# Latent heads: the inverse roots spread over rows by one split-format product, high and low parts in rows 0 and 32 with zero rows between

## The chip, the cores and the metric

The kernel runs on one core of one Trainium2 chip. The metric is the device time of one launch in microseconds (us), lower is better. A core has five engines with queues of their own: PE (TensorE, matrix products; its weight loads are listed as PEld), DVE (VectorE), ACT (ScalarE), POOL (GpSimd) and SP (SyncE, which here only issues DMAs). They meet by semaphores. The tensor engine has two clock levels, 1.2 and 2.4 GHz; the profile gives the granted clock as a share of the full one, so 0.50 is 1.2 GHz and 1.00 is 2.4 GHz.

## The reference, cut to what matters

The program is two transformer blocks and a hybrid block on 512 tokens of width 1024, about 2.3 ms in all. The change is inside one mixer of the first block, the latent attention of 8 heads (64 plain and 32 rotated features a head, 96 in all):

```
q  = (rms_norm(c_q, cq_norm) @ w_uq).reshape(B, S, H, dn + dr)
kv = (rms_norm(c_kv, ckv_norm) @ w_ukv).reshape(B, S, H, dn + dv)
k  = concatenate([kv[..., :dn], broadcast_to(k_rope[:, :, None, :], (B, S, H, dr))], axis=-1)
v  = kv[..., dn:]
q  = rms_norm(q, q_norm)            # one inverse root per token and head, over 96 features
k  = rms_norm(k, k_norm)
q  = concatenate([q[..., :dn], rope(q[..., dn:], pos)], axis=-1)
k  = concatenate([k[..., :dn], rope(k[..., dn:], pos)], axis=-1)
return causal_block_attention(q, k, v).reshape(B, S, H * dv)
```

## The kernel before, in words

The program is a row of stages, each a block in which every engine has a list of its own; a stage ends when all engines are through, semaphores are cleared, and the next begins. Nothing of one stage overlaps with the next, apart from DMAs that nobody has waited for yet. Around the change stand three stages: the attention `ev_nsa` (during which SP loads the constants and weights of the next one, in `fill`), then `ev_latent_heads` (function `latent_heads`), then the attention `ev_mla`, which needs all that `latent_heads` leaves: queries in `xnT`, keys in `ev_km`, values in `ev_vm`.

In `latent_heads` features lie on partitions and the 512 tokens along the free axis. Products go one after another into the 8 banks of `PS`; product number n uses bank n % 8, and the semaphore `made` counts them. The order is written out by hand on each engine:

- PE: products 0 to 7 make raw q (four plain, two rotated) and two of k; product 8 sums the squares of q per head, with a 0/1 matrix `pick`, into 8 rows; 9 to 14 make the rest; product 15 sums the squares of k. Products 16 to 21 (`spread_out(0, w)`) take the 8 rows of inverse roots `rs` of q and spread them over 128 rows by the 0/1 matrix `spread`, one for each of the six tiles of q. Product 22 is the first tile of values (`value(0)`), 23 to 28 spread the roots of k (`spread_out(1, w)`), 29 to 31 are the other three tiles of values.
- ACT squares, copies k out of the banks, and for each of the two sums (`power`) takes exp(-0.5 ln(x)); at the end it copies the four value tiles (`take_v`).
- DVE refines each root by one Newton step (`newton`, three instructions on 8 rows), and multiplies: `qo` and `ko` are the rotated parts, `nope` the plain parts, two half-height instructions for each tile.
- SP moves the rotated rows from `qo` to `xnT` and from `ko` to `ev_km`, 8 DMAs each, and waits for all 16.
- A bank is used again only when its reader is done: `spread_out(1, m)` waits for `q_done`, `value(1)` for all of `nope` of q, `value(3)` for `k_roped`.

A product of two f32 operands appears as two matmul records. Elsewhere the kernel uses a split format: f32 data is rounded to fp32r (the high part), the rest (f32 minus high) is rounded to fp32r as the low part, and products run on fp32r operands, each one matmul record (`split_product`, L555 to L557). `low_alias` gives an fp32r tile that lies on the memory of the tile allocated last.

Of the kernel before, what the change touches and what calls it, by code (L numbers as in the profile page):

```python
# [26 lines left out]
P = 128  # L27
# [3 lines left out]
EPS = 1e-6  # L31
# [1650 lines left out]
NH, HD = 8, 64  # L1682
CMP_L, CMP_S = 32, 16
# [41 lines left out]
def head_of_row():  # L1725
# [7 lines left out]
    return pick  # L1733

# [12 lines left out]
def mixer_even(nc, C, D, x, xnT):  # L1747
    with ExitStack() as mem:
# [204 lines left out]
        pick, spread = sb("pick", [P, 6, NH]), sb("spread", [NH, 6, P])  # L1953
# [39 lines left out]
        with ExitStack() as m3:  # L1993
            km, vm = sb("km", [P, NH, SEQ], m3), sb("vm", [P, NT, 512], m3)
            filled = 16 * sum(1 + rows.shape[0] // P for rows in C.made_rows.values())
            latent_heads(nc, C, cq, ckv, kr, uq, ukv, gm, cosT, sinT, turn, pick, spread, xnT, km, vm, loaded, filled)
# [279 lines left out]
def latent_heads(nc, C, cq, ckv, kr, uq, ukv, gm, cosT, sinT, turn, pick, spread, qm, km, vm, loaded, filled):  # L2276

    N = MQK
    with ExitStack() as mem, stage(nc, "ev_latent_heads", "zeroed made squared q_copied k_copied q_cos k_cos k_sin k_turned q_sin "
# [29 lines left out]
        def _(pe):  # L2309
# [27 lines left out]
            def spread_out(i, w):  # L2337
                nc.tensor.matmul(bank(), spread[:, w], rs[:, i], start=True, stop=True).then_inc(s["made"], 1)
# [12 lines left out]
            sums = bank()[0:NH]  # L2351
# [18 lines left out]
            sums = bank()[0:NH]  # L2370
            for m in range(4):
                nc.tensor.matmul(sums, pick[:, m], sq[:, 6 + m], start=m == 0, stop=False)
            nc.tensor.matmul(sums, C.ones[0:ROT, 0:NH], sq[0:ROT, 10], start=False, stop=True).then_inc(s["made"], 1)

            pe.wait_ge(s["q_rstd"], 1)
# [25 lines left out]
        def _(act):  # L2401
# [7 lines left out]
            def power(n, i):  # L2409
                act.wait_ge(s["made"], n + 1)  # L2410
                nc.scalar.activation(rs[:, i], PS[0:NH, n % 8, :], ACT.Ln, bias=ec[0:NH, 0:1], scale=1.0 / N).then_inc(s["logged"], 1)
# [7 lines left out]
            act.wait_ge(s["zeroed"], 1)  # L2419
            for m in range(4):  # L2420
# [17 lines left out]
        def _(dve):  # L2438
            step = Steps(dve, s["steps"])

            def newton(n, i, done):
                dve.wait_ge(s["exped"], i + 1)
                y, t = rs[:, i], tt[:, i]
                step(nc.vector.scalar_tensor_tensor(out=t, in0=PS[0:NH, n % 8, :], scalar=N * EPS, in1=y, op0=ALU.add, op1=ALU.mult))
                step(nc.vector.scalar_tensor_tensor(out=t, in0=t, scalar=-0.5 / N, in1=y, op0=ALU.mult, op1=ALU.mult))
                nc.vector.scalar_tensor_tensor(out=y, in0=t, scalar=1.5, in1=y, op0=ALU.add, op1=ALU.mult).then_inc(done, 1)
# [1235 lines left out]
```

## Time and profile before

| | |
|---|---|
| median of three timed runs | 2325.05 us (2324.07 to 2329.28) |
| profiled execution, its time | 2320.53 us |
| profiled execution, its span | 2319.0 us |
| mean granted clock of the tensor engine | 0.935 |
| busy: PE / DVE / ACT / POOL | 89% / 55% / 43% / 8% of the span |
| the stage `latent_heads` | from 304.0 to about 360.0 us of the span |

Times in a trace count from the start of the span. A busy share is an average over stages with different limits. A timeline row gives start, duration and, in brackets, how long the engine had been idle and who ended it; a row with x12 covers twelve instructions in one stretch. Matmuls overlap with their neighbours in the pipeline, so the step from one to the next is shorter than the duration of one.

### The profile page before, as it was taken

The page shows a single profiled execution, that of the slowest core. Times are in us where ns is not written, and L with a number is a line of the kernel's source. Part 1 is how long each engine was busy: PE and PEld are TensorE (multiplying, and loading weights), DVE is VectorE, ACT ScalarE, POOL GpSimd, SP SyncE. Part 2 cuts the span into 40 slices and gives each one's busy share as a digit, 9 for nine tenths or more (in the row PEclk, how much of TensorE's full clock was granted, in tenths as well). Part 3 has the DMA queues.
Part 4 walks back from the last instruction along what each step waited for, and adds up shares of the span by engine and source line. Part 5 has one row for each costly group of instructions (what it writes and reads, how often), then busy time and mean ns, then how long its engine had stood idle before and what let it go on. Part 6 is the DMA issues. An engine that isn't in the chain of part 4 may idle for free. (4 is left out here: it accounts for less than half of the span.)

```text
span 2319.0 us, 31287 instructions
## 1 busy us (share of the span) xinstructions
PE 2068.7 (89%) x11611; PEld 1570.0 (68%) x11611; DVE 1285.5 (55%) x1814; ACT 994.2 (43%) x1308; POOL 185.8 (8%) x182
## 2 busy tenths in 40 slices
PE   7966898889999989997899999997898789686998
PEld 5743334668888877876777888786476359575776
DVE  3367746353133234444566666888367745525888
ACT  2135736342223222221566665774243643404774
POOL 0010000000000000000311010111112200002111
PEclk9978988989999999997899999999999789886999
DMA  8006101144144125002778777995320000126996
GB/s 249 6 14 237 47 10 45 37 127 123 43 122 127 37 83 194 1 37 83 256 269 282 278 270 281 370 391 216 88 73 28 12 1 1 74 84 174 399 373 258
DMA packets 220713, 336.29 MB, mean 145 GB/s; under 512 B 50413, under 2 KB 135309, under 8 KB 220606
## 3 DMA queue, kind: packets, MB, share of 16 engines
q1 hardware_dynamic: 213470, 314.53, 40.0%
q0 software_dynamic: 7136, 20.34, 2.3%
q8 instruction: 66, 1.08, 0.2%
q14 instruction: 41, 0.34, 0.0%
HBM read 306.82 MB, written 26.95 MB: 144 GB/s over the span
## 5 line engine op out<-in xcount | busy, mean ns | idle before, releaser
L1526 DVE TENSOR_TENSOR moe_pass_wL<-moe_pass_w,moe_pass_wH 128x2048 fp32r<-128x2048 f32 (+1 forms) x144 | 303.4, 2112 | 115.8 <-ACT moe_pass_wH L1450 111.3
L1450 ACT ACTIVATE moe_pass_wH<-moe_pass_w 128x2048 fp32r<-128x2048 f32 (+1 forms) x144 | 254.7, 1772 | 129.6 <-PE PS L557 97.2
L555 PE MATMUL PS<-moe_pass_wL,moe_pass_xgH 128*128 128x512 f32 (+1 forms) x384 | 148.3, 386 | 9.1 <-DVE moe_pass_xgL L1531 4.8
L1526 DVE TENSOR_TENSOR hm_pass_wL<-hm_pass_w,hm_pass_wH 128x2048 fp32r<-128x2048 f32 x60 | 135.9, 2288 | 34.8 <-ACT hm_pass_wH L1450 34.7
L555 PE MATMUL PS<-xnT_low,ffn_upH 128*128 128x512 f32 x352 | 140.3, 399 | 7.4 <-DVE xnT_low L873 7.1
L557 PE MATMUL PS<-moe_pass_wH,moe_pass_xgH 128*128 128x512 f32 (+1 forms) x384 | 143.5, 374 | 0.0
L556 PE MATMUL PS<-moe_pass_wH,moe_pass_xgL 128*128 128x512 f32 (+1 forms) x384 | 143.5, 374 | 0.0
L557 PE MATMUL PS<-ffn_xH,ffn_upH 128*128 128x512 f32 x352 | 139.9, 397 | 0.0
L556 PE MATMUL PS<-ffn_xH,ffn_up_low 128*128 128x512 f32 x352 | 138.4, 393 | 0.0
L1450 ACT ACTIVATE hm_pass_wH<-hm_pass_w 128x2048 fp32r<-128x2048 f32 x60 | 112.2, 1910 | 17.1 <-PEq L1340 6.0
L880 DVE TENSOR_TENSOR ffn_hT<-ffn_sg,PS 128x512 f32<-128x512 f32 x22 | 15.1, 688 | 167.7 <-PE PS L557 167.7
L839 ACT ACTIVATE ffn_sg<-PS 128x512 f32<-128x512 f32 x22 | 13.2, 599 | 187.8 <-PE PS L557 187.8
L555 PEld LDWEIGHTS PS<-moe_pass_wL,moe_pass_xgH 128*128 128x128 f32 x384 | 72.5, 189 | 28.5 <-issue 11.8
L555 PE MATMUL PS<-xnT_low,od_in_wH 128*128 128x512 f32 x192 | 77.3, 403 | 7.1 <-DVE od_W_low L689 7.1
L555 PEld LDWEIGHTS PS<-xnT_low,ffn_upH 128*128 128x128 f32 x352 | 66.6, 189 | 22.4 <-DVE ffn_up_low L858 7.3
L557 PEld LDWEIGHTS PS<-moe_pass_wH,moe_pass_xgH 128*128 128x128 f32 x384 | 72.6, 189 | 10.6
L556 PEld LDWEIGHTS PS<-moe_pass_wH,moe_pass_xgL 128*128 128x128 f32 x384 | 72.7, 189 | 9.4
L557 PEld LDWEIGHTS PS<-ffn_xH,ffn_upH 128*128 128x128 f32 x352 | 66.9, 190 | 15.9
L556 PEld LDWEIGHTS PS<-ffn_xH,ffn_up_low 128*128 128x128 f32 x352 | 66.7, 190 | 15.8
L556 PE MATMUL PS<-od_xH,od_W_low 128*128 128x512 f32 x192 | 76.7, 399 | 0.0
L555 PE MATMUL PS<-hm_pass_wL,hm_pass_xgH 128*128 128x512 f32 x160 | 65.3, 408 | 12.7 <-DVE hm_pass_wL L1526 7.1
L557 PE MATMUL PS<-od_xH,od_in_wH 128*128 128x512 f32 x192 | 75.7, 394 | 0.0
(841 smaller groups left out, 4868.6 us busy)
## 6 DMA issues: line engine op xcount, KB each, us to landing
moe_pass_w<-in_moe_w_down SPq DMA_DIRECT2D x40, 1024.0 KB, 4.9
moe_pass_w<-in_moe_w_gate SPq DMA_DIRECT2D x32, 1024.0 KB, 5.2
moe_pass_w<-in_moe_w_up SPq DMA_DIRECT2D x32, 1024.0 KB, 7.2
hm_pass_w<-in_exp_w_gate SPq DMA_DIRECT2D x40, 512.0 KB, 7.7
hm_pass_w<-in_exp_w_up SPq DMA_DIRECT2D x40, 512.0 KB, 6.9
hm_pass_w<-in_exp_w_down SPq DMA_DIRECT2D x40, 512.0 KB
od_W<-in_od_w_in SPq DMA_DIRECT2D x12, 1024.0 KB, 8.2
moe_pass_w<-in_moe_w_gate SPq DMA_DIRECT2D x16, 768.0 KB
```

The costliest lines, as they stand in the source:

```text
L555: nc.tensor.matmul(out, lh, rl, start=start, stop=False)
L556: nc.tensor.matmul(out, ll, rh, start=False, stop=False)
L557: return nc.tensor.matmul(out, lh, rh, start=False, stop=stop)
L839: nc.scalar.activation(sg[:, c % 2], PS[:, c % 2, :], ACT.Silu).then_inc(s["silu"], 1)
L880: nc.vector.tensor_tensor(hT[:, c], sg[:, c % 2], PS[:, 2 + c % 2, :], ALU.mult).then_inc(s["hidden"], 1)
L1450: nc.scalar.activation(wH[:, i % S, 0:n], w[:, i % R, 0:n], ACT.Copy).then_inc(s["high"], 1)
L1526: nc.vector.tensor_tensor(wL[:, i % S, 0:n], w[:, i % R, 0:n], f32(wH[:, i % S, 0:n]), ALU.subtract) \
```

## The change

The inverse roots are kept in 40 rows instead of 8: the 0/1 matrix `pick` now has 40 columns, in which columns 32 to 39 repeat columns 0 to 7, so `rs` holds the 8 roots twice, in rows 0 to 7 and 32 to 39, and rows 8 to 31 get the inverse root of the constant alone. `newton` gets two instructions more: rows 0 to 39 are rounded to fp32r in a new tile `both`, and then rows 32 to 39 of it are overwritten with f32 minus rounded. `both` is cleared first on POOL. The matrix `spread` now has 128 rows, with its 8 rows at 0 and at 32 and zeros elsewhere, and ACT rounds it once into `heads` at the start of the stage. Each of the twelve spreading products then is one product of two fp32r operands with 128 rows. On DVE the second `newton` stands after two of the four `nope` of q, not ahead of them. The two constants are loaded at their new sizes.

```diff
+def sums_twice():
+    pick = np.zeros((P, 6, SUMS), np.float32)
+    for a in (0, LOW):
+        pick[:, :, a:a + NH] = head_of_row()
+    return pick.reshape(P, 6 * SUMS)
+
+def spread_twice():
+    spread = np.zeros((P, 6, P), np.float32)
+    for a in (0, LOW):
+        spread[a:a + NH] = head_of_row().transpose(2, 1, 0)
+    return spread.reshape(P, 6 * P)
...
-        pick, spread = sb("pick", [P, 6, NH]), sb("spread", [NH, 6, P])
+        pick, spread = sb("pick", [P, 6, SUMS]), sb("spread", [P, 6, P])
+        heads = low_alias(nc, "ev_spread_high", [P, 6, P])
...
-        rs, tt, ec = sb("rs", [NH, 2, SEQ]), sb("tt", [NH, 2, SEQ]), sb("ec", [P, 1])
+        rs, tt, ec = sb("rs", [SUMS, 2, SEQ]), sb("tt", [SUMS, 2, SEQ]), sb("ec", [P, 1])
+        both = mem.enter_context(nc.sbuf_tensor("lh_both", [P, 2, SEQ], F32R))
+        high, low = slice(0, SUMS), slice(LOW, SUMS)
...
+            step(nc.gpsimd.memset(f32(both[:, :, :]), 0.0))
...
             def spread_out(i, w):
-                nc.tensor.matmul(bank(), spread[:, w], rs[:, i], start=True, stop=True).then_inc(s["made"], 1)
+                nc.tensor.matmul(bank(), heads[:, w], both[:, i], start=True, stop=True).then_inc(s["made"], 1)
...
+            pe.wait_ge(s["spread"], 1)
             pe.wait_ge(s["q_rstd"], 1)
             spread_out(0, 4)
...
             act.wait_ge(s["zeroed"], 1)
+            act.wait_ge(loaded["rope"], 80)
+            nc.scalar.activation(heads[:, :, :], spread[:, :, :], ACT.Copy).then_inc(s["spread"], 1)
...
-                nc.vector.scalar_tensor_tensor(out=y, in0=t, scalar=1.5, in1=y, op0=ALU.add, op1=ALU.mult).then_inc(done, 1)
+                step(nc.vector.scalar_tensor_tensor(out=y, in0=t, scalar=1.5, in1=y, op0=ALU.add, op1=ALU.mult))
+                dve.wait_ge(s["zeroed"], 2)
+                step(nc.vector.tensor_copy(both[high, i], y))
+                nc.vector.tensor_tensor(both[low, i], rs[low, i], f32(both[low, i]), ALU.subtract).then_inc(done, 1)
...
-            newton(15, 1, s["k_rstd"])
             for m in range(4):
                 nope(18 + m, 0, m, qr, qm, s["q_done"])
+                if m == 1:
+                    newton(15, 1, s["k_rstd"])
```

On DVE, in the second half of the stage, stands before the change (L2481 makes `qo`, L2444 to L2446 are `newton`, L2455 is `nope`, L2488 makes `ko`):

```order
L2481 TENSOR_TENSOR lh_qo<-lh_qa,PS 128x512 x2
L2444 SCALAR_TENSOR_TENSOR lh_tt<-PS,lh_rs 8x512
L2445 SCALAR_TENSOR_TENSOR lh_tt<-lh_tt,lh_rs 8x512
L2446 SCALAR_TENSOR_TENSOR lh_rs<-lh_tt,lh_rs 8x512
L2455 SCALAR_TENSOR_TENSOR xnT<-lh_qn,ev_gm,PS 64x512 x8
L2488 TENSOR_TENSOR lh_ko<-lh_ka,PS 128x512 x2
L2455 SCALAR_TENSOR_TENSOR ev_km<-lh_kn,ev_gm,PS 64x512 x8
```

And in the changed kernel, at the same place:

```order
L2508 TENSOR_TENSOR lh_qo<-lh_qa,PS 128x512 x2
L2482 SCALAR_TENSOR_TENSOR xnT<-lh_qn,ev_gm,PS 64x512 x4
L2468 SCALAR_TENSOR_TENSOR lh_tt<-PS,lh_rs 40x512
L2469 SCALAR_TENSOR_TENSOR lh_tt<-lh_tt,lh_rs 40x512
L2470 SCALAR_TENSOR_TENSOR lh_rs<-lh_tt,lh_rs 40x512
L2472 CAST lh_both<-lh_rs 40x512
L2473 TENSOR_TENSOR lh_both<-lh_rs,lh_both 8x512
L2482 SCALAR_TENSOR_TENSOR xnT<-lh_qn,ev_gm,PS 64x512 x4
L2516 TENSOR_TENSOR lh_ko<-lh_ka,PS 128x512 x2
L2482 SCALAR_TENSOR_TENSOR ev_km<-lh_kn,ev_gm,PS 64x512 x8
```

The second `newton` moved behind four of the eight half-height multiplications of q, and is two instructions longer.

On PE the order of the products stays; the last rows of the stage read before the change (L2372 and L2373 sum the squares of k, L2338 is `spread_out`, L2335 `value`):

```order
L2372 MATMUL PS<-lh_sq,ev_pick 8x512 x4
L2373 MATMUL PS<-lh_sq,ones 8x512
L2338 MATMUL PS<-lh_rs,ev_spread 128x512 x6
L2335 MATMUL PS<-ev_ukv,ev_latent 128x512
L2338 MATMUL PS<-lh_rs,ev_spread 128x512 x6
L2335 MATMUL PS<-ev_ukv,ev_latent 128x512 x3
```

And in the changed kernel:

```order
L2393 MATMUL PS<-lh_sq,ev_pick 40x512 x4
L2394 MATMUL PS<-lh_sq,ones 40x512
L2359 MATMUL PS<-lh_both,ev_spread_high 128x512 x6
L2356 MATMUL PS<-ev_ukv,ev_latent 128x512
L2359 MATMUL PS<-lh_both,ev_spread_high 128x512 x6
L2356 MATMUL PS<-ev_ukv,ev_latent 128x512 x3
```

Nothing moved here; the operands of the twelve spreading products changed, and the sums have 40 rows.

## Rows read from the trace of the kernel before

**Rows 1.** Windows over the stage: length, busy time (x instructions) of each engine, granted clock, DMA.

```profile
332.00:336.00 4.00, 4.00 (x10) 1.31 (x9) 1.31 (x2) 2.50 (x3) 0.00 (x0) 1.00 0.00 0
336.00:340.00 4.00, 4.00 (x6) 1.67 (x5) 3.81 (x7) 0.09 (x1) 0.00 (x0) 0.50 0.41 96
...
356.00:360.00 4.00, 3.38 (x4) 0.77 (x3) 0.00 (x0) 1.78 (x3) 0.00 (x0) 0.52 0.00 0
```

**Rows 2.** Timeline of PE from the first spreading product to the next stage.

```profile
333.37 8.06 PE L2338 MATMUL PS<-lh_rs,ev_spread 8*128 8x512 f32 x12
341.35 2.08 PE L2335 MATMUL PS<-ev_ukv,ev_latent 128*128 128x512 f32 x2
343.36 10.61 PE L2338 MATMUL PS<-lh_rs,ev_spread 8*128 8x512 f32 x12
353.89 5.49 PE L2335 MATMUL PS<-ev_ukv,ev_latent 128*128 128x512 f32 x6
360.86 2.62 PE L391 MATMUL PS<-ev_km,xnT 96*128 96x128 f32 x10 [1.48 <-PEq L42]
363.59 0.33 PE L404 MATMUL PS<-ident,ev_mla_pn 128*128 128x128 f32 x1
```

**Rows 3.** Timeline of DVE in the same stage.

```profile
330.05 1.22 DVE L2477 TENSOR_TENSOR lh_qa<-lh_qa,lh_qb 128x1024 f32<-128x1024 f32 x1
334.59 1.48 DVE L2481 TENSOR_TENSOR lh_qo<-lh_qa,PS 128x512 f32<-128x512 f32 x2 [3.32 <-PE PS L2338]
336.12 0.68 DVE L2444 SCALAR_TENSOR_TENSOR lh_tt<-PS,lh_rs 8x512 f32<-8x512 f32 x1
...
338.16 6.18 DVE L2455 SCALAR_TENSOR_TENSOR xnT<-lh_qn,ev_gm,PS 64x512 f32<-64x512 f32 x8
...
354.00 1.52 DVE L2455 SCALAR_TENSOR_TENSOR ev_km<-lh_kn,ev_gm,PS 64x512 f32<-64x512 f32 x2 [0.18 <-PE PS L2338]
```

**Rows 4.** Timeline of ACT in the same stage.

```profile
306.98 0.63 ACT L2422 ACTIVATE lh_sq<-lh_qn 128x512 f32<-128x512 f32 x1 [9.47 <-DVE lh_qn L2460]
...
335.46 0.63 ACT L2413 ACTIVATE lh_rs<-lh_rs 8x512 f32<-8x512 f32 x1
...
359.42 0.60 ACT L2417 ACTIVATE ev_vm<-PS 128x512 f32<-128x512 f32 x1 [1.11 <-PE PS L2335]
```

**Rows 5.** SP's DMA issues (timeline), and from issue to landing for L2304.

```profile
224.79 10.29 SPq L1980 DMA_DIRECT2D hm_pass_made<-ev_TcT  x8
346.25 4.95 SPq L2304 DMA_DIRECT2D ev_km<-lh_ko  x8
DMA to landing us min/median/max: 1.9/2.0/2.1
```

**Rows 6.** Timeline of PE in an earlier stage: neighbouring products of fp32r operands.

```profile
60.10 0.39 PE L555 MATMUL PS<-xnT_low,ev_ring 128*128 128x512 f32 x1
60.33 0.39 PE L556 MATMUL PS<-ev_yT_low,ev_W_low 128*128 128x512 f32 x1
```

**Rows 7.** Groups by line and shape: busy us, mean ns of one, idle before.

```profile
L2262 DVE COPY xnT<-ev_front 64x2048 f32<-64x2048 f32 x1 | 1.2, 1225 | 0.0
L617 DVE TENSOR_TENSOR ev_yT_low<-ev_yT,ev_out_yH 128x512 fp32r<-128x512 f32 x8 | 5.5, 686 | 1.4 <-ACT ev_out_yH L596 1.4
L673 ACT ACTIVATE ev_ring<-ev_W 128x1024 fp32r<-128x1024 f32 x11 | 11.6, 1057 | 64.5 <-PE PS L557 64.5
L2295 POOL MEMSET xnT<- 32x2048 f32 x1 | 1.8, 1797 | 0.1
```

**Rows 8.** Start of the attention `ev_nsa`: PE's timeline, and a window with its clock.

```profile
188.11 4.84 PE L391 MATMUL PS<-ev_front,xnT 128*128 128x128 f32 x10 [2.29 <-PEq L42]
192.78 0.27 PE L404 MATMUL PS<-ident,ev_nsa_pn 128*128 128x128 f32 x1
188.00:192.00 4.00, 3.89 (x8) 2.62 (x9) 2.60 (x9) 1.31 (x5) 0.00 (x0) 0.50 0.53 160
```

**Rows 9.** A window inside the attention `ev_mla`.

```profile
384.00:388.00 4.00, 2.30 (x10) 1.12 (x11) 3.37 (x12) 3.52 (x12) 0.00 (x0) 0.90 0.00 0
```

More of the change, by code:

```diff
@@ L1682 @@
 NH, HD = 8, 64
+LOW, SUMS = 32, 40
 CMP_L, CMP_S = 32, 16
@@ L1995, in mixer_even @@
             filled = 16 * sum(1 + rows.shape[0] // P for rows in C.made_rows.values())
-            latent_heads(nc, C, cq, ckv, kr, uq, ukv, gm, cosT, sinT, turn, pick, spread, xnT, km, vm, loaded, filled)
+            latent_heads(nc, C, cq, ckv, kr, uq, ukv, gm, cosT, sinT, turn, pick, spread, heads, xnT, km, vm, loaded, filled)
             jobs = []
@@ L2273, in _, with latent_heads @@
             nc.vector.tensor_copy(pcT[:, :, :], PS[:, 6:8, :])
-def latent_heads(nc, C, cq, ckv, kr, uq, ukv, gm, cosT, sinT, turn, pick, spread, qm, km, vm, loaded, filled):
+def latent_heads(nc, C, cq, ckv, kr, uq, ukv, gm, cosT, sinT, turn, pick, spread, heads, qm, km, vm, loaded, filled):
     N = MQK
-    with ExitStack() as mem, stage(nc, "ev_latent_heads", "zeroed made squared q_copied k_copied q_cos k_cos k_sin k_turned q_sin "
+    with ExitStack() as mem, stage(nc, "ev_latent_heads", "zeroed spread made squared q_copied k_copied q_cos k_cos k_sin k_turned q_sin "
                                    "q_turned logged exped steps q_rstd k_rstd q_roped k_roped q_done k_done v_taken moved") as (block, s):
@@ L2350, in _ @@
             pe.wait_ge(s["q_copied"], 1)
-            sums = bank()[0:NH]
+            sums = bank()[high]
             for w in range(6):
@@ L2369, in _ @@
             pe.wait_ge(s["squared"], 11)
-            sums = bank()[0:NH]
+            sums = bank()[high]
             for m in range(4):
                 nc.tensor.matmul(sums, pick[:, m], sq[:, 6 + m], start=m == 0, stop=False)
-            nc.tensor.matmul(sums, C.ones[0:ROT, 0:NH], sq[0:ROT, 10], start=False, stop=True).then_inc(s["made"], 1)
+            nc.tensor.matmul(sums, C.ones[0:ROT, high], sq[0:ROT, 10], start=False, stop=True).then_inc(s["made"], 1)
+            pe.wait_ge(s["spread"], 1)
             pe.wait_ge(s["q_rstd"], 1)
@@ L2410, in power @@
                 act.wait_ge(s["made"], n + 1)
-                nc.scalar.activation(rs[:, i], PS[0:NH, n % 8, :], ACT.Ln, bias=ec[0:NH, 0:1], scale=1.0 / N).then_inc(s["logged"], 1)
+                nc.scalar.activation(rs[:, i], PS[high, n % 8, :], ACT.Ln, bias=ec[high, 0:1], scale=1.0 / N).then_inc(s["logged"], 1)
                 act.wait_ge(s["logged"], i + 1)
@@ L2443, in newton @@
                 y, t = rs[:, i], tt[:, i]
-                step(nc.vector.scalar_tensor_tensor(out=t, in0=PS[0:NH, n % 8, :], scalar=N * EPS, in1=y, op0=ALU.add, op1=ALU.mult))
+                step(nc.vector.scalar_tensor_tensor(out=t, in0=PS[high, n % 8, :], scalar=N * EPS, in1=y, op0=ALU.add, op1=ALU.mult))
                 step(nc.vector.scalar_tensor_tensor(out=t, in0=t, scalar=-0.5 / N, in1=y, op0=ALU.mult, op1=ALU.mult))
-                nc.vector.scalar_tensor_tensor(out=y, in0=t, scalar=1.5, in1=y, op0=ALU.add, op1=ALU.mult).then_inc(done, 1)
+                step(nc.vector.scalar_tensor_tensor(out=y, in0=t, scalar=1.5, in1=y, op0=ALU.add, op1=ALU.mult))
+                dve.wait_ge(s["zeroed"], 2)
+                step(nc.vector.tensor_copy(both[high, i], y))
+                nc.vector.tensor_tensor(both[low, i], rs[low, i], f32(both[low, i]), ALU.subtract).then_inc(done, 1)
             def gained(dst, src, col, other_):
@@ L3633 @@
 CONSTANTS = {"bucket_table": bucket_table, "rope_table": rope_tables, "rope_spread": rope_spread,
-             "head_pick": lambda: head_of_row().reshape(P, 6 * NH),
-             "head_spread": lambda: head_of_row().transpose(2, 1, 0).reshape(NH, 6 * P),
+             "head_pick": sums_twice, "head_spread": spread_twice,
              "ones_row": lambda: np.ones((1, NH), np.float32), "wkv_masks": wkv_masks, "chunk_restart": chunk_restart}
```

## Prediction, made before the changed kernel ran

> **What bounds the kernel now.** I read the timeline of the stage first, because a stage with a barrier behind it is worth exactly the time of whichever engine is last in it. PE is that engine. From its first spreading product at 333.37 it has no gap until the last value product [rows 2], and in the windows from 332 to 340 it is busy 4.00 of 4.00 us [rows 1]. DVE, which has as much to do with its multiplications, ends at 354.00 + 1.52 = 355.52 [rows 3]; ACT takes the last value tile from 359.42 to 360.02 [rows 4], and that is the end of the stage. The next stage's first product follows 0.84 us later, at 360.86 [rows 2].
>
> Then the clock. In 332 to 336 the granted clock is 1.00, in 336 to 340 it is 0.50, and it is still 0.52 in 356 to 360 [rows 1]: the engine ran at 1.2 GHz from about 336 on although it never paused. What it did ahead of the fall were products with 8 rows of operand (8\*128, 8x512). What it did ahead of the rise, which must lie at about 360 since the next stage starts at full speed, were products with 128 rows. The price is plain: six spreading products are 12 records and cost 333.37 to 341.35, 7.98 us, in the first group, which began at 2.4 GHz, and 343.36 to 353.89, 10.53 us, in the second, all at 1.2 GHz (1.75 each) [rows 2]. One value product costs 2.01 us there (341.35 to 343.36), the last three 5.49 [rows 2]. DVE waits for PE: at the last tile of k it had 0.18 us of idle time ahead of it [rows 3].
>
> So the end hangs on 12 spreading products (18.5 us) and 4 value products (7.5 us), on a PE at half clock. The rest of the program lies behind a barrier and moves with the end of this stage.
>
> **The change, part by part.**
>
> *Spreading products.* Two neighbouring fp32r products stand 0.23 us apart at full clock (60.10, 60.33) [rows 6]. Their cost does not depend on the rows used: the 8-row records here are as far apart as those of the 128-row values (1.75 for two records against 5.49 / 3 = 1.83 with the tail). So twelve products fall from 18.5 us to 12 x 0.23 = 2.8 us at full clock, or double that, 5.5 us, at half. PE stops being the last engine, and what matters is who is next: DVE.
>
> *First Newton step.* It gains a rounding of 40x512 and a subtraction of 8x512. The subtraction is a TENSOR_TENSOR of 512 elements per row, 0.69 us [rows 7]. No row rounds to fp32r on DVE. The lower bound is a plain copy from SBUF at 1.225 us for 2048 elements, a quarter of which is 0.31; the upper is that it runs like the TENSOR_TENSOR, 0.69 [rows 7]. I take 0.45, nearer the copy, as it has one source and a fixed part. With 0.05 for the two hand-overs the step is longer by about 1.2 us. The DVE work behind it, which ended at 330.05 + 1.22 = 331.27 [rows 3], then ends at 332.5. The spreading starts at 333.37, as PE is busy until then, so this is hidden with 0.9 us to spare; at the upper bound still with 0.7. The roots of q are ready earlier still on the same list, so they are hidden too.
>
> *The constant rounded on ACT.* 128x768: between 128x512 and 128x1024 at 1.057 us [rows 7], so about 0.8 us. ACT has nothing to do until 306.98 [rows 4], the stage opens at 304.0: free, 2 us to spare. If the cover were gone it would cost its 0.8.
>
> *POOL.* The memset of 1024 elements per row costs about half of 1.797, 0.9 us [rows 7]. The two memsets behind it end near 308.7 instead of 307.8, and their rows are first written by others at 334 and later. Free.
>
> *Loads.* `pick` grows from 128x48 to 128x240 values, `spread` from 8x768 to 128x768: 24 + 24 KB become 120 + 384 KB, under half a megabyte more. They stand early in the load queue of `ev_nsa`; all of its transfers are issued by 224.79 + 10.29 = 235.1 [rows 5], 69 us ahead of the stage. SP issues as many DMAs as before. Free.
>
> *40 instead of 8 rows or columns.* ACT and DVE instructions take their time from the elements per row (8x512 takes 0.68, as 128x512 does [rows 3]), and the matmuls stream the same 512 columns. Zero.
>
> *The new chain on DVE.* The first `qo` started 334.59 - 333.37 = 1.22 us after its product did, for two records [rows 2, 3]. One record less is half of that: 0.6, so `qo` starts at 333.97. From there I add, with durations of [rows 3]:
>
> - two `qo`, 1.48: to 335.45
> - four `nope` halves, 6.18 / 2 = 3.09: to 338.54
> - second Newton step; its input from ACT is there at 335.46 + 0.63 = 336.09 [rows 4], so no wait. 338.16 - 336.12 = 2.04, plus 1.2: to 341.78
> - four `nope` halves, 3.09: to 344.87
> - two `ko`, TENSOR_TENSOR like the `qo` and the one of [rows 7], 1.40: to 346.27
> - eight `nope` halves of k, 4 x 1.53 = 6.12: to 352.4
>
> DVE does not wait in between: the k spreading begins when `k_rstd` comes at 341.8, six products at 0.46 each are made by 344.6, and the first is needed at 344.87. The last of them and `value(1)` wait for the last `nope` of q, 344.87.
>
> *The others' ends.* PE: three value products from 344.9, at half clock 5.49 us, to 350.4, and 0.9 us more for ACT to take the last: 351.3. SP: first `ko` at 345.6, the last issue some 4.3 us on, landing 2.0 us later [rows 5]: 351.9. DVE is last at 352.4. Moving the Newton step behind two tiles of q costs nothing, as the chain is one list on one engine; it only makes k later (341.8 and not 338.7) and q earlier.
>
> *Sum in the stage.* 360.02 - 352.4 = 7.6 us less.
>
> *What is given back.* PE now idles from about 336 (six products and one value product) to 341.8, and again from 350.4 to the next stage at 352.4 + 0.84 = 353.2. Before, the last value products ran on until 359.4 and the attention opened at 2.4 GHz: from its first product to its first transposition 363.59 - 360.86 = 2.73 us. The other attention, `ev_nsa`, opened at clock 0.50, and there the same stretch took 192.78 - 188.11 = 4.67 us [rows 8]. The difference, 1.94 us, is my price of a cold opening; it is a little high, as `ev_nsa` has more work for DVE in a unit. I expect the cold opening.
>
> Here a rule of the Trainium skill ("TensorE: Matmul & The Clock Gate", "Why this matters for your kernels") can be weighed: idle gaps between bursts bring the half clock, and a busy engine is released from it. For the kernel before the trace does not agree with the second half: 4.00 of 4.00 us busy at 0.50. By the rule alone the kernel before would have had no half clock here to lose, and the change, which makes gaps, could only lose by it.
>
> **Sum.** 7.6 - 1.9 = 5.7 us. The profiled execution goes from 2320.53 to 2314.8. The median of the timed runs lies 4.5 us above the profiled one, so against it: 2325.05 - 5.7 = 2319.4 us, 0.25% less.
>
> **The rivals.**
>
> 1. *More is given back than a cold opening* (chance 0.30, time 2321 to 2325, no change that can be told). For it: the attention itself pauses often enough to lose the clock now and then; in 384 to 388 PE was busy 2.30 of 4.00 us and the mean clock was 0.90, so it fell inside the window [rows 9], and everything behind the stage is shifted by some 6 us against whatever sets these falls. If the cold opening lasts twice as long, 3.8 us go, and 3.8 are left. Against it: in `ev_nsa` it was over within 4.7 us.
> 2. *The attention opens warm* (chance 0.12, time 2317.4). The three values run 5.2 us on 128 rows without a pause, the same thing that stood ahead of the rise at 360, and only 3 us of idling follow. Then all 7.6 us stay.
> 3. *Slower, by a cold attention* (chance 0.05, time about 2334 at worst). One mechanism: the attention, entered at 1.2 GHz, does not get out. A cold us costs 1.94 / 4.67 = 0.42 us; the 7.6 us are used up after 18 us of cold attention, and with 40 us of it cold the loss is 17, so 9 us slower. For it: the clock stood at 0.50 in this stage under a busy engine [rows 1]. Against it: those were 8-row operands, and the attention's have 96 or 128 rows; `ev_nsa`, entered at 0.50, got out. The same page of the Trainium skill ("A second HAM failure mode: psum-queue depth-cycling") describes a kernel whose short idles between groups make the clock go back and forth; the trace agrees that this attention has such a fall [rows 9].
> 4. *The change does little, since PE was not what the end hung on* (chance 0.04, time 2324). DVE would end at 352.4 only if nothing holds it; if the rounding or the wait for cleared rows cost 3 us more than I think, 3 us of the gain go. The rows speak against it: 2 us of slack at each place.
>
> **How the numbers follow.** My forecast, 5.7 us less with a cold opening, has 0.49. A measurement of this kernel tells about 0.2% (4.65 us) from no change. Faster by more: forecast and rival 2, less a part for scatter about the bound that is only 1 us away: 0.58. Within 0.2%: rivals 1 and 4 and that part: 0.37. Slower: 0.05. The forecast's own range is rounding 0.31 to 0.69 (0.14 us and 0.24 us to either side, in one place on the path), opening 1.2 to 2.7: 2318.5 to 2320.4. To hold 8 in 10 it must reach to rival 2 and through rival 1, and carry the scatter of the timed runs (1 us below, 4 us above their median): 2315.5 to 2325.
>
> **What the changed profile would show.** Right: spreading products of one record, 0.23 to 0.46 us apart; DVE without a wait from 334 to 352.4, and last in the stage; PE idle from 336 to 342; the next stage's first product at 353.2 instead of 360.86; clock 0.50 in its first us and 1.00 within 5. Wrong: DVE waiting for PE anywhere behind 334; the rounding at more than 0.7 us; PE waiting for DVE ahead of 333.4; a clock that stays at 0.50 behind 360; or, in the sum, a part of the gain that is there at the end of this stage and gone at the end of the program.

## The result, and the profile after

The changed kernel takes 2310.61 us (median of 5 runs, 2303.26 to 2312.46); the kernel before, in turn with it, 2324.07 (5 runs, 2315.34 to 2329.28). The ratio is 0.9942, 95% interval 0.9917 to 0.9967. That is faster by 0.6%, where I had forecast 0.25% and a range whose fast end was 2315.5 us. The profiled execution took 2310.61, its span is 2309.1 at a mean granted clock of 0.937; before it was 2319.0.

First the stage of the change. PE's timeline of the changed kernel (start, length, line, operands, count, [idle before <- releaser]):

```profile
333.28 1.67 PE L2359 MATMUL PS<-lh_both,ev_spread_high 128*128 128x512 f32 x6
334.79 1.02 PE L2356 MATMUL PS<-ev_ukv,ev_latent 128*128 128x512 f32 x2
341.54 2.93 PE L2359 MATMUL PS<-lh_both,ev_spread_high 128*128 128x512 f32 x6 [5.73 <-DVE lh_both L2473]
344.66 3.52 PE L2356 MATMUL PS<-ev_ukv,ev_latent 128*128 128x512 f32 x6 [0.19 <-DVE xnT L2482]
352.90 5.03 PE L391 MATMUL PS<-ev_km,xnT 96*128 96x128 f32 x10 [4.71 <-PEq L42]
357.72 0.42 PE L404 MATMUL PS<-ident,ev_mla_pn 128*128 128x128 f32 x1
```

The spreading products are single records and take 1.67 and 2.93 us where they took 8 and 10.5 [rows 2]. From the second group on PE waits for DVE and no longer the other way round. DVE's timeline:

```profile
326.40 0.42 DVE L2472 CAST lh_both<-lh_rs 40x512 fp32r<-40x512 f32 x1
326.86 0.68 DVE L2473 TENSOR_TENSOR lh_both<-lh_rs,lh_both 8x512 fp32r<-8x512 f32 x1
...
333.89 1.28 DVE L2508 TENSOR_TENSOR lh_qo<-lh_qa,PS 128x512 f32<-128x512 f32 x2 [1.46 <-PE PS L2359]
335.09 3.08 DVE L2482 SCALAR_TENSOR_TENSOR xnT<-lh_qn,ev_gm,PS 64x512 f32<-64x512 f32 x4
...
344.63 1.28 DVE L2516 TENSOR_TENSOR lh_ko<-lh_ka,PS 128x512 f32<-128x512 f32 x2
345.84 6.19 DVE L2482 SCALAR_TENSOR_TENSOR ev_km<-lh_kn,ev_gm,PS 64x512 f32<-64x512 f32 x8
```

The rounding costs 0.42 us, DVE runs without a wait from 333.89 to 352.03 and is last. The next stage's first product starts at 352.90 instead of 360.86 [rows 2]. The windows with the granted clock (length, busy and count of PE, PEld, DVE, ACT, POOL, then clock, DMA share, GB/s):

```profile
336.00:340.00 4.00, 0.00 (x0) 0.00 (x0) 3.83 (x6) 0.49 (x2) 0.00 (x0) 0.91 0.46 108
340.00:344.00 4.00, 2.46 (x6) 1.82 (x6) 3.80 (x7) 0.00 (x0) 0.00 (x0) 0.50 0.07 17
344.00:348.00 4.00, 3.81 (x8) 1.41 (x6) 3.90 (x6) 1.19 (x2) 0.00 (x0) 0.74 0.20 47
348.00:352.00 4.00, 0.18 (x1) 0.00 (x0) 3.84 (x6) 0.60 (x1) 0.00 (x0) 1.00 0.36 85
352.00:356.00 4.00, 3.10 (x7) 2.27 (x8) 1.58 (x7) 1.11 (x5) 0.00 (x0) 0.61 0.50 173
356.00:360.00 4.00, 4.00 (x11) 2.38 (x10) 2.86 (x12) 2.67 (x8) 0.00 (x0) 0.53 0.90 339
360.00:364.00 4.00, 2.98 (x15) 1.65 (x14) 3.18 (x10) 4.00 (x14) 0.00 (x0) 1.00 0.05 18
```

The attention opens at 1.2 GHz, and from its first product to its first transposition are 4.82 us (352.90 to 357.72) where there were 2.73. So far all is as forecast. Here the gain is 363.59 - 357.72 = 5.87 us. A part of it, 0.2 us, was there ahead of the stage: from the stage's first product to the attention's it takes 48.87 us where it took 56.66, 7.79 us less.

To see where the other 5 us come from I subtracted the start times of the same DVE instruction in two profiles, all along the program. Each row begins with the place in the kernel before; the numbers are the shifts of the others against it, each from one profile (the kernels are those of the next section; "before again" is a second profile of the kernel before):

```
place (us)                     after   again1  again2  old order  awake  delay  f32rows  before again
 294.9 ahead of the stage      -0.2    -0.5    -1.7    -1.2       -1.2   +1.1   -1.0     +0.6
 365.9 attention has begun     -5.9    -6.3    -7.6    -6.1       -8.7   +2.9   -7.3     +0.6
 486.6 attention is over       -7.2    -7.6    -9.0    -7.6       -7.9   +1.4   -6.5     +0.6
1941.2                         -3.5    -8.9    -8.7    -4.1      -11.6   +5.0   -1.1     +0.3
2085.5 router of the last MoE  -9.7   -14.0   -15.2   -10.9      -12.4   -1.8   -1.7     +0.5
```

Between 486 and 1941 shifts come and go by up to 5.4 us, in either direction. Between 1941 and 2085 they don't scatter: five of the six kernels with the split format gain 5.1 to 6.8 us there (9.7 - 3.5 = 6.2 in the changed kernel), in code that the change doesn't touch, and the two with f32 products in this table 0.6 or less. Behind 2085 the shifts drift again: from there to the last DVE instructions (at 2314.9 in the kernel before) the changed kernel gains 0.2 us more, and the others of this table lose 0 to 3.9 us. The timeline of that router before (L195 transposes the tokens, L204 multiplies with the router's weights):

```profile
2065.62 2.24 SPq L2652 DMA_DIRECT2D hm_br<-in_router_eb  x1
2070.39 4.87 DVE L179 SCALAR_TENSOR_TENSOR hm_xs<-x,hm_norm_ss,hm_gx 128x1024 f32<-128x1024 f32 x4 [4.33 <-DMA hm_br<-in_router_eb]
2071.74 3.68 PE L195 MATMUL PS<-ident,hm_xs 128*128 128x128 f32 x16 [4.39 <-DVE hm_xs L179]
2075.21 3.44 PE L204 MATMUL PS<-hm_wr,xnT 128*128 128x20 f32 x16
2080.22 3.44 PE L204 MATMUL PS<-hm_wr,xnT 128*128 128x20 f32 x16
```

and after:

```profile
2062.10 0.81 SPq L2680 DMA_DIRECT2D hm_br<-in_router_eb  x1
2065.62 4.87 DVE L179 SCALAR_TENSOR_TENSOR hm_xs<-x,hm_norm_ss,hm_gx 128x1024 f32<-128x1024 f32 x4 [3.03 <-DMA hm_br<-in_router_eb]
2066.95 3.34 PE L195 MATMUL PS<-ident,hm_xs 128*128 128x128 f32 x16 [3.08 <-DVE hm_xs L179]
2070.13 1.94 PE L204 MATMUL PS<-hm_wr,xnT 128*128 128x20 f32 x16
2072.87 1.86 PE L204 MATMUL PS<-hm_wr,xnT 128*128 128x20 f32 x16
```

The issue of one small load takes 0.81 us instead of 2.24, the token scaling that waits for it starts 3.52 us behind that issue instead of 4.77, and then the same sixteen products take 1.94 and 1.86 us instead of 3.44. Their windows, before:

```profile
2070.00:2074.00 4.00, 2.26 (x11) 2.27 (x12) 3.61 (x4) 0.26 (x1) 0.00 (x0) 0.50 0.94 259
2074.00:2078.00 4.00, 4.00 (x21) 4.00 (x20) 1.27 (x2) 1.92 (x4) 0.00 (x0) 0.50 0.97 355
```

and after:

```profile
2066.00:2070.00 4.00, 3.04 (x15) 3.05 (x16) 4.00 (x4) 1.04 (x2) 0.00 (x0) 0.57 0.98 259
2070.00:2074.00 4.00, 4.00 (x38) 4.00 (x37) 1.18 (x2) 1.73 (x4) 0.00 (x0) 1.00 1.01 409
```

What lengthens the issue? The DMA queues over the 2.3 us from that issue on, in the kernel before (2065.6 to 2067.9; packets, MB, share):

```profile
q1 hardware_dynamic: 2157, 0.12, 62.3%
q8 instruction: 1, 0.02, 2.5%
```

and over the 2.9 us from it on in the changed one (2062.1 to 2065):

```profile
q1 hardware_dynamic: 2354, 0.31, 74.9%
```

A load of instructions falls on it before. After, that load is at 2072.4, here in the window 2071 to 2074:

```profile
q8 instruction: 1, 0.02, 2.0%
```

The change moves it: a product in the split format is one MATMUL and one weight load, where an f32 product is two of each. In the first part of the profile's page PE has 11611 products and as many weight loads before, and after:

```profile
PE 2052.6 (89%) x11599; PEld 1565.9 (68%) x11599; DVE 1286.9 (56%) x1818; ACT 994.7 (43%) x1309; POOL 188.3 (8%) x183
```

12 + 12 instructions less and one wait more: PE's list is 23 shorter. If the load is one of PE's instructions, a fixed count of them after the last, it now comes at a later place of the program. That was the theory for the last three experiments.

This load is not the only one that lies beside a long issue. In the kernel before one comes at 1123.29, and an issue of `moe_pass_w <- in_moe_w_up` at 1123.77 takes 2.32 us, where the median of the 48 of its line is 0.37.

### The profile page after: what moved, and what is told of

It reads as the page before. It is cut to its first block and busy times, and to the rows that moved or that the text cites. A ratio compares the mean times of both kernels' runs of the same rounds, so it can differ in the third digit from the quotient of the medians.

```text
span 2309.1 us, 31272 instructions
## 1 busy us (share of the span) xinstructions
PE 2052.6 (89%) x11599; PEld 1565.9 (68%) x11599; DVE 1286.9 (56%) x1818; ACT 994.7 (43%) x1309; POOL 188.3 (8%) x183
## 5 line engine op out<-in xcount | busy, mean ns | idle before, releaser
L555 PE MATMUL PS<-moe_pass_wL,moe_pass_xgH 128*128 128x512 f32 (+1 forms) x384 | 148.5, 387 | 10.5 <-DVE moe_pass_wL L1526 5.6
```

Source lines behind the costliest of these rows:

```text
L555: nc.tensor.matmul(out, lh, rl, start=start, stop=False)
```

## Experiments

Each kernel ran in turn with the kernel before on one chip. "Less" is the mean of the runs against the mean of the kernel before, with a 95% interval; the ratio is a second estimate from the same runs and can differ from that of the means by 0.001. Single runs of one kernel scatter by 3.3 to 5.4 us (standard deviation), so three more measurements of unaltered kernels belong to the evidence.

**The changed kernel again, twice.** No edit.

> The changed kernel unaltered, for more pairs with the kernel before. Its first profile showed 5.9 us gained at the first transposition of the latent attention and 9.9 us at the end of the span; the difference came 1000 us later, where the clock was low for other stretches. Theory 'local': what the change does is the 5.9 us, the rest is scatter of the clock between executions, so the ratio is 0.9975 and the interval takes in 0.9970 to 0.9980. Rival 'place': the earlier start moves later stages against what sets the clock, in every execution alike, so the ratio is 0.994 again (13 us) and the low stretches of the clock in the profile are the same as in the first profile of this kernel.

> The changed kernel unaltered once more. So far its runs, with those of the old order, lie 8 to 14 us below the kernel before, and its profiles show 7.2 us of it by 612 us of the span. Theory 'local': 7.2, ratio 0.9969. Rival: 10 us or more, ratio below 0.9957, with the later stages gaining 3 us in each profile.

8.2 +- 2.4 us less (12 runs; ratio 0.9966, 0.9951 to 0.998) and 14.7 +- 3.8 less (6 runs; 0.9938, 0.9917 to 0.9959). With the first 5 runs (14.0 +- 5.5) these are 23, and their mean is 11.2 +- 2.0 us less. The three measurements differ among themselves by up to 6.5 us, so a part of the 14 us of the first may be luck; the gain is larger than the 5.7 forecast all the same.

**The kernel before again.** No edit.

> The kernel before unaltered, as the kernel under test: it shows what a comparison of twelve executions tells of no change at all, and gives a second profile of it. Ratio 1.000, interval about 0.0015 to either side. The stage takes the same 56.7 us (first product of the stage to first product of the attention) as in the first profile, with clock 0.50 from about 336 to 360 again. The time at the end of the span may differ from the first profile by 5 us, from stages behind 1000 us. If the stage differs by more than 0.5 us between the two profiles, what I called local is scatter too.

0.1 +- 3.7 us more; ratio 0.9996 (0.998 to 1.0013). The stage takes 56.74 us (304.74 to 361.48) as before, 56.66: what is told of a stage to a tenth holds from run to run.

**The order alone,** in the kernel before.

```
-            newton(15, 1, s["k_rstd"])
             for m in range(4):
                 nope(18 + m, 0, m, qr, qm, s["q_done"])
+                if m == 1:
+                    newton(15, 1, s["k_rstd"])
```

> The kernel before with the second Newton step moved behind two tiles of q, nothing else. PE is the last engine of the stage and the roots of k are needed at 343.4, while DVE would have them by about 341.5 even in the new order: no change of the stage's end, ratio 1.000. Rival: half of the gain comes from the order, then 3 us less. In the profile the next stage starts at 360.7 to 361.

2.6 +- 2.7 us less; ratio 0.9983 (0.9968 to 0.9998). In the profile the shift is -0.3 us ahead of the stage and -0.3 behind it: the order alone does nothing in the stage. That the ratio's interval ends just below 1 is no gain of the stage; the shift is still -0.1 at 800 us.

**The old order,** in the changed kernel (the same edit undone).

> The changed kernel with the second Newton step ahead of the four tiles of q, as before the change. DVE's list is the same work without a wait either way, so the stage ends within 0.3 us of the changed kernel (attention starts 48.9 us after the stage opens); k's roots come 3.1 us earlier, PE's second group of spreading starts at 338.4, values later in the list wait for q as before. Rival: the move is worth something, and the stage is 1 us or more longer here.

12.4 +- 3.5 us less (5 runs); ratio 0.9958 (0.9936 to 0.9979). The stage takes 49.83 us (302.91 to 352.74), the changed kernel's 48.87 (304.03 to 352.90): with short products the order is worth 0.96 us in the stage, which the total can't tell. I had expected 0.3 at most. The second Newton step now comes before ACT has the roots of k, and DVE waits:

```profile
334.93 0.68 DVE L2468 SCALAR_TENSOR_TENSOR lh_tt<-PS,lh_rs 40x512 f32<-40x512 f32 x1 [0.87 <-ACT lh_rs L2435]
```

**f32 products with 128 rows,** in the kernel before: rows 8 to 127 of both operands are zero, no split format, the old order. The products and their number stay. Left out of the edit below are the constant of 128 rows a wait of ACT for the cleared rows and, on ACT and DVE, the rows 0 to 7 written out.

```
-        pick, spread = sb("pick", [P, 6, NH]), sb("spread", [NH, 6, P])
+        pick, spread = sb("pick", [P, 6, NH]), sb("spread", [P, 6, P])
...
-        rs, tt, ec = sb("rs", [NH, 2, SEQ]), ...
+        rs, tt, ec = sb("rs", [P, 2, SEQ]), ...
...
+            step(nc.gpsimd.memset(rs[:, :, :], 0.0))
```

> The kernel before with f32 spreading products of 128 rows instead of 8: the spreading matrix and the roots have zero rows 8 to 127, two records for each product as before. Theory '8-row operands cost the clock': the clock stays at 1.00 through the stage, twelve products take 12 x 0.86 = 10.3 us instead of 18.5 and the four values 3.4 instead of 7.5; PE would be through at 347 or a little later and DVE, which has 1.2 us less for each Newton step than in the changed kernel, ends the stage at about 350; the attention opens warm, so 9 to 11 us less. Rival 'zero rows do not count as work': the clock falls at 336 as before and the stage takes as long as before, ratio 1.000. A third: the clock falls for another reason ahead of 336 (sums with 8 columns), same result as the rival.

5.7 +- 2.6 us less; ratio 0.9968 (0.9955 to 0.998). Its windows and PE's timeline:

```profile
336.00:340.00 4.00, 4.00 (x10) 1.72 (x10) 3.87 (x6) 0.60 (x1) 0.00 (x0) 1.00 0.44 102
340.00:344.00 4.00, 4.00 (x11) 1.74 (x10) 3.84 (x7) 0.00 (x0) 0.00 (x0) 1.00 0.05 12
332.28 5.42 PE L2339 MATMUL PS<-lh_rs,ev_spread 128*128 128x512 f32 x12
338.39 5.31 PE L2339 MATMUL PS<-lh_rs,ev_spread 128*128 128x512 f32 x12
351.56 5.04 PE L391 MATMUL PS<-ev_km,xnT 96*128 96x128 f32 x10 [5.29 <-PEq L42]
```

The clock stays at 2.4 GHz, the second group takes 5.31 us instead of 10.53 [rows 2], PE keeps ahead of DVE, and the stage is as short as with the split format (48.45 us; shift from -1.0 to -7.3 us). What cost the time before was the clock, and the number of products alone was no bound. Two things missed what I expected: the attention opened cold (4.83 us to its first transposition) and not warm, and the total is 5.7 us and not 9 to 11.

**64 and 32 rows** (the same with fewer rows of the operands used), one execution each.

```
-                nc.tensor.matmul(bank(), spread[:, w], rs[:, i], ...
+                nc.tensor.matmul(bank(), spread[0:64, w], rs[0:64, i], ...
```

> The f32 kernel with spreading products of 64 rows instead of 8 or 128, one look at the clock. If what counts is how many rows have data in the operand's shape, 64 may stand on either side: clock 1.00 through 336 to 344 means that half the rows are enough, 0.50 that they are not. With 1.00 the stage ends as with 128 rows (attention starts 48.4 us after the stage opens), with 0.50 near 56.7 as before.

> The f32 kernel with spreading products of 32 rows, one look at the clock. 64 and 128 rows kept the clock at 1.00 through the stage, 8 rows lost it at 336. If it is the rows with data that count, 32 stand between: 1.00 through 336 to 344, or 0.50 as with 8.

With 64 rows:

```profile
340.00:344.00 4.00, 4.00 (x11) 1.82 (x11) 3.84 (x6) 0.60 (x1) 0.00 (x0) 1.00 0.20 47
```

With 32 rows:

```profile
336.00:340.00 4.00, 4.00 (x7) 1.51 (x6) 3.84 (x6) 0.59 (x1) 0.00 (x0) 0.56 0.35 82
340.00:344.00 4.00, 4.00 (x6) 0.99 (x5) 3.84 (x6) 0.07 (x1) 0.00 (x0) 0.50 0.21 49
```

PE is busy 4.00 of 4.00 us in all three. After products with 32 rows the clock fell as with 8, with 64 it stayed as with 128, though the rows from 8 on held zeros. The next stage's first product came at 361.32 with 32 rows and at 352.88 with 64.

**A warm opening:** five f32 products without use behind the last value product, in the changed kernel and in the one with 128 rows.

```
             value(3)
+            pe.wait_ge(s["k_roped"], 2)
+            for _ in range(5):
+                nc.tensor.matmul(PS[:, 0, :], ukv[:, 0:P], ckv, start=True, stop=True)
```

> The changed kernel with five more f32 products of 128 rows on PE behind the last value product, into a bank that is no longer read; nobody waits for them and they use no result. They fill about 348.2 to 352.5, where PE idled. If the cold opening of the attention costs 1.9 us, the attention opens at clock 1.00 and its first transposition comes 2.7 instead of 4.8 us after its first product: 2 us less than the changed kernel. If the clock is low there for another reason, nothing changes against the changed kernel. If the products run on past the end of the stage, they cost what they overrun.

> The f32 kernel with 128 rows (zero rows, no split format, old order) and five more f32 products on PE behind the last value product. If the clock is a matter of what PE does, it stays at 1.00 from 304 through the opening of the attention: first transposition of the attention 2.7 us behind its first product, and at that point 8.5 to 9 us ahead of the kernel before, as much as the changed kernel with the same five products (8.5). The ratio then is 0.9965 or lower; scatter of the later clock is larger than the difference to the changed kernel. Rival: the products themselves hold up the stage's end, 1 us later than without them.

7.0 +- 3.4 us less (0.9973, 0.9954 to 0.9992) and 6.9 +- 2.7 (0.9974, 0.996 to 0.9988), neither ahead of the changed kernel. With the five products the changed kernel's opening is warm:

```profile
352.15 2.62 PE L391 MATMUL PS<-ev_km,xnT 96*128 96x128 f32 x10 [0.89 <-PEq L42]
354.88 0.33 PE L404 MATMUL PS<-ident,ev_mla_pn 128*128 128x128 f32 x1
```

2.73 us against 4.82, so the cold opening does cost 2.1. But the shift, -8.7 us at the opening, is -7.9 when the attention is over, while the changed kernel goes from -5.9 to -7.2 there. The falls of the clock inside the attention stand at other places there, and most of it is gone. With 128 rows the clock held through the attention's first 50 us, and the shift at 486 was -11.1; the issue in its router was as long as before, 2.48 us (below).

**The stage as long as before,** with the split format: ten idle multiplications on DVE at its end.

```
+            for _ in range(10):
+                step(nc.vector.tensor_tensor(kb[:, :], ka[:, :], ka[:, :], ALU.mult))
```

> The changed kernel with ten f32 multiplications of 128x512 on DVE at the end of the stage (7.2 us, of results that nobody reads), so that the attention starts where it did before the change, but cold. Theory 'local' (a us in this stage is a us of the program, the rest is scatter): 7.2 us slower than the changed kernel, so 2 us about the kernel before, ratio 0.999 to 1.001. Rival 'the changed kernel gains elsewhere, whatever its position': ratio about 0.997 or less. In the profile: the first product of the attention 7.2 us later than in the changed kernel.

3.3 +- 3.0 us less (0.9988, 0.9971 to 1.0005). The stage takes 56.52 us. Against its own shift ahead of the stage it stands at +1.8 at the opening and +0.3 at 486: nothing is gained there. The router gives 6.8 us all the same. So those 6 us are not the stage's. The total shows less than 6.8; in the profile 3.6 us were lost between 486 and 1941 and 2.9 behind the router, in stretches where all kernels drift.

**The place of the instruction load.** Three kernels change the length of PE's list: the changed one with 24 and with 12 instructions more, all waits long fulfilled, ahead of the first spreading product (from ahead of the stage to the attention's opening they gain 5.8 and 5.9 us, the changed kernel 5.7, so the waits cost nothing there); and the kernel before with 4 less, which leaves the rotary part of the keys out of their norm.

```
-            pe.wait_ge(s["spread"], 1)
+            for _ in range(49):        # 25 in the second kernel
+                pe.wait_ge(s["spread"], 1)
```

```
             for m in range(4):
-                nc.tensor.matmul(sums, pick[:, m], sq[:, 6 + m], start=m == 0, stop=False)
-            nc.tensor.matmul(sums, C.ones[0:ROT, 0:NH], sq[0:ROT, 10], start=False, stop=True).then_inc(s["made"], 1)
+                ins = nc.tensor.matmul(sums, pick[:, m], sq[:, 6 + m], start=m == 0, stop=m == 3)
+            ins.then_inc(s["made"], 1)
```

> The changed kernel with 48 more waits on `spread`, long fulfilled, ahead of the first spreading product: 24 more instructions in TensorE's list (two waits stand in one), no work, 5 us ahead of the product that waits for lh_both in any case. Theory (a), the place of the instruction load: the new list is 23 instructions shorter than the one before, because a split-format product is one record where an f32 product is two, and so the 16 KB instruction load of the router of the last MoE comes 10 us later and misses the issue of hm_br. With 24 instructions back the load is at the issue again: hm_br <- in_router_eb takes 1.8 to 2.5 us instead of 0.66 to 0.84, hm_xs starts 1.3 us later, and if the clock's gain there hangs on it, the 6 us gained between 1941 and 2085 us are gone: mean 5 to 6 us less gained than the changed kernel (-5 to -6 instead of -11). Theory (b), chance in the clock's later stretches: issue 0.66 to 0.84 us as in all six kernels with the split format, gain -11 us +-3. The stage latent_heads takes 48.9 us in both.

> The same with 24 such waits, 12 instructions: the list is 11 shorter than before. The kernel with the products that keep the clock up was 3 shorter and its load came late, the kernels before were 0 shorter and it came early. So by (a) this one still has the short issue (0.66 to 0.84 us) and the changed kernel's gain of about 11 us; it is the control for what the waits themselves cost. If waits themselves cost anything, both padded kernels lose alike.

> The kernel before with the fifth product of the keys' sums left out (the rotary part of the keys is not in their norm): 4 instructions less in TensorE's list, nothing else. By (a) the load comes after the issue: hm_br 0.66 to 0.84 us, hm_xs 1.3 us earlier after that issue begins, and where the clock follows, 5 to 6 us gained between 1941 and 2085 us; the stage latent_heads is up to 1 us shorter. By (b) the issue stays at 1.8 to 2.5 us and the mean differs by no more than 1 us from the kernel before.

With 24 more: 7.3 +- 2.9 us less (12 runs; 0.9966, 0.9951 to 0.9981). The issue is long again, an instruction load is beside it, and the products are slow:

```profile
2059.40 2.06 SPq L2681 DMA_DIRECT2D hm_br<-in_router_eb  x1
2064.03 4.87 DVE L179 SCALAR_TENSOR_TENSOR hm_xs<-x,hm_norm_ss,hm_gx 128x1024 f32<-128x1024 f32 x4 [4.25 <-DMA hm_br<-in_router_eb]
2068.85 3.44 PE L204 MATMUL PS<-hm_wr,xnT 128*128 128x20 f32 x16
```

With 12 more: 12.2 +- 3.6 us less (9 runs; 0.9957, 0.9943 to 0.9972), the issue and the products as in the changed kernel:

```profile
2052.63 0.96 SPq L2681 DMA_DIRECT2D hm_br<-in_router_eb  x1
2056.36 4.87 DVE L179 SCALAR_TENSOR_TENSOR hm_xs<-x,hm_norm_ss,hm_gx 128x1024 f32<-128x1024 f32 x4 [3.24 <-DMA hm_br<-in_router_eb]
2060.97 1.86 PE L204 MATMUL PS<-hm_wr,xnT 128*128 128x20 f32 x16
```

Between 1941 and 2085 the first has a shift from -6.3 to -6.4, the second from -12.6 to -19.0. Both drift back behind it, to +0.7 and -15.6 at the end, so the single profiles don't give the totals.

The kernel with 4 less has other keys and computes something else. Its total (2358.84 us, ratio 1.0147, 1.0126 to 1.0169) is no measure: it has 11769 products on PE instead of 11611 and falls behind only past 2250 us, which would fit tokens that go to other experts, though I did not follow them. Its router runs the same instructions as before, and between 1941 and 2085 its shift goes from -4.7 to -10.9:

```profile
2060.86 0.80 SPq L2652 DMA_DIRECT2D hm_br<-in_router_eb  x1
```

All sixteen profiles, by the length of PE's list against the kernel before (R is the time from the issue of the first of the two `hm_br` loads, `hm_br <- in_router_gb`, to the start of DVE's last copy to `xnT` in this router; "issue" is the one of the second, `hm_br <- in_router_eb`):

```
list                             kernels                                issue of hm_br   R
+20                              128 rows, awake                        2.48             18.4
+1                               24 more waits                          2.06             21.2
 0                               before, again, order, 128, 64, 32 rows 1.83 to 2.24     20.8 to 21.3
-3                               changed, awake                         0.75             20.3
-4                               before with one product less           0.80             15.1
-11                              12 more waits                          0.96             15.2
-23                              changed, again twice, old order, delay 0.66 to 0.84     14.9 to 15.2
```

The length of the list separates the issues in all sixteen: from 0 on they are long, from -3 down short. So does the place of the load: in the eight with the long issue an instruction load starts 0.4 to 0.8 us behind the start of the issue, in the eight with the short one 9.9 to 10.5 us behind it. The list separates the clock in fourteen. The other two are those with the idle products: in the changed kernel the issue is short and the clock stays at 0.50, in the one with 128 rows the issue is long and the products still take 2.17 and 2.45 us instead of 3.44.

## Why the prediction was wrong

**The stage was right.** DVE last at 352.03 (forecast 352.4), next stage at 352.90 (353.2), the gain there 7.96 us, of which 0.17 came ahead of the stage (7.6). It is no luck: from ahead of the stage to the attention's opening the five profiles with this stage (the changed kernel's three and the two with more waits) gain 5.7 to 5.9 us. Rounding 0.42 (0.45), constant on ACT 0.84 (0.8), memset, wider operands and loads all hidden as forecast. Of the 0.37 us that DVE was sooner, 0.2 come from the pair of `qo`, which takes 1.28 and not 1.48. One term was off where it didn't count: I had the last three value products at half clock until 350.4, but the clock rose within 344 to 348 (0.74), they took 3.52 us instead of 5.49, and PE was through at 348.2. Two readings are off without weight: the 0.68 us of an instruction with 128x512 elements stands in [rows 7] (686 ns) and not in [rows 3], and rival 4 claims 2 us of slack at each place, where the second Newton step, on a list without a wait, has none.

**The cold opening was right in place and size,** 4.82 - 2.73 = 2.1 us (1.9), and perhaps wrong as a balance: a part of it seems to be made up inside the attention. The changed kernel got 1.3 us back by 486, the delayed one 1.5 of its 1.8, the other five with the split format and a cold opening 0.7 to 1.6, and the kernel without a cold opening gave 0.8 away. Against it: the f32 kernel with 128 rows opens cold too and lost 0.8, and the kernel with the order alone, whose stage and opening are as before, lost 1.3; so drift of this size is there too, and no run separates the two. At the attention's end 7.0 us stand (7.2 less the 0.2 from ahead of the stage), and I had 5.7.

**The step that failed** is the sentence "The rest of the program lies behind a barrier and moves with the end of this stage." It was true for work and waits and false for the places of instruction loads. These depend on the number of instructions in the list, which the change makes 23 less. One load sat beside the issue of `hm_br <- in_router_eb`, 1700 us on. Moved away, it let the token scaling start 1.25 us sooner (4.77 - 3.52), and the clock then rose in the router, where it had stayed at 0.50: together 5 to 7 us. 7.0 + 6.2 = 13.2 us, of which the drift between and behind takes some: 11.2 +- 2.0 in the mean of 23 runs, 5.5 more than forecast. The experiment that puts the instructions back gives 7.3, against 12.2 with half of them: this is what is left without the load's move, near to the forecast 5.7. The two totals differ by 4.9 +- 4.0 us, so it is the profiles, more than the totals, that settle it. The change moves the other instruction loads of PE too; what they cost or give elsewhere no run separates.

**The rivals.** Rival 1 (more given back) did not come: the attention gave back less, not more. Rival 2 (warm) did not come by itself, and made by hand it brought no gain that the totals could tell (7.0 +- 3.4 against 8.2 +- 2.4). Rival 3's mechanism, an attention that doesn't get out of the half clock, never showed; it got out by 360. Rival 4 is refuted by the timeline. Only rival 2 lay on the side where the truth was, and by no more than 1.9 us: I had no case for a gain of its own outside the stage. And the lower end of the range, with 1 us of scatter from three runs, was too near for a kernel whose single runs have a standard deviation of 3.3 to 5.4 us; the five of the result reach 8.7 us below their median.

**The half clock under a busy engine.** With 8 and 32 rows PE was busy all of the time at 0.50, with 64 and 128 rows at 1.00. This speaks against the rule of the Trainium skill ("TensorE: Matmul & The Clock Gate", "Why this matters for your kernels") that a busy PE is let go of the half clock, as the rows before did. By the rule alone the kernel with 128 rows would have gained nothing; it gained 6.3 us in the stage with the attention's opening.

**What stays open.** Why the load of PE's instructions makes an issue on SP take over 1 us longer, I only saw, not explained; that both use the same DMA engines is an argument, not shown. And why a start of `hm_xs` 5.20 us behind the first `hm_br` issue (changed kernel, awake) left the clock low, when 5.08 us (12 more waits) let it rise, and why it rose in part after 6.34 us in the kernel with 128 rows, awake, no run tells. So the step from a sooner start to a higher clock rests on fourteen profiles that agree and two that don't.

## What to carry to other kernels

Products with few rows of operand can cost twice, though PE has no gap: look at the granted clock in the windows of a busy stretch, and if it is 0.50 there, try zero rows up to 64 or 128, which sufficed here, before a new format. Where PE then no longer sets the end, further shortening of its products buys nothing in the stage. An edit that changes the number of instructions of an engine moves that engine's instruction loads in all that follows; look for a gain or a loss far behind the edit by subtracting start times of the same instructions, and repeat it with empty instructions that restore the count before you credit the edit.

## What the hardware showed that I had not expected

- The granted clock fell under a PE that was busy 4.00 of 4.00 us with 8 or 32 rows of f32 operands, and stayed at 1.00 with 64 or 128 rows of which 8 held something other than zero. The number of rows is not all: in the router before, PE is busy 4.00 of 4.00 us at 0.50 (2074 to 2078) with transpositions and with products of 128 rows and 20 columns, and in the changed kernel the same products ran at 1.00.
- Instructions are loaded while the program runs. The profile's page of the changed kernel counts them (below). With one of them beside it, the issue of `hm_br` took 1.83 to 2.48 us instead of 0.66 to 0.96:

```profile
q8 instruction: 66, 1.08, 0.2%
```

One section of the Trainium skill ("Trainium Architecture — The Big Picture", "The software stack") has the instruction streams brought into the engines when the program is loaded. That is at most a part of it: the trace has 66 loads of 16 KB on this queue between the first and the last instruction.
- A cold opening cost 2.1 us at the attention's first transposition. By the attention's end seven kernels with it had 0.7 to 1.6 us of that back; one lost 0.8, so this may be drift.
